# Residual rows of fifteen output tiles added by an accumulating DMA instead of by VectorE

## The reference, cut to what matters

```python
h = rms_norm(x, g_norm) * (1 + scale) + shift
p = h @ w_in                              # h_A, B_A, C_A, z_A, u_B, v_B, z_B, each 512 wide
s = c_a * h_a
y_a = b_a * dwconv3(s) * silu(z_a)
v_n = layer_norm(v_b, g_v, b_v)
y_b = u_b * chunk_spatial_mix(v_n, w_s, b_s) * silu(z_b)
y = concatenate([y_a, y_b]) @ w_out
out = rms_norm(x + gate * y, g_final)     # x is read a second time here: the residual
```

## Time and profile before

| what | before |
|---|---|
| median of 3 runs | 339.34 us |
| the profiled execution | 339.12 us |
| its span, slowest core (core 4) | 337.3 us (other cores 334.1 to 337.1) |
| TensorE busy | 284.2 us, 84% |
| VectorE busy | 187.7 us, 56% |
| ScalarE busy | 114.1 us, 34% |
| GpSimd busy | 110.7 us, 33% |
| TensorE's granted clock, mean of the core | 0.968 |

### The profile page before, as it was taken

The page is one execution under the profiler, slowest core; times in us unless marked ns, Lnnn a source line. Parts: engine busy times, 40 slices in busy tenths (PEclk is TensorE's granted clock), DMA queues, the critical chain, the costliest instruction groups (busy, mean ns, idle before and its releaser), DMA issues.

```text
span 337.3 us, 5476 instructions; the slowest of 8 cores (334.1 to 337.3 us)
## 1 busy us (share of the span) xinstructions
PE 284.2 (84%) x1696; PEld 147.6 (44%) x1720; DVE 187.7 (56%) x350; ACT 114.1 (34%) x206; POOL 110.7 (33%) x161
## 2 busy tenths in 40 slices
PE   0325539999899999998989999999999999999840
PEld 0222214444454444443445454445555557766420
DVE  0321015445564454277887857658864666668982
ACT  2611013206552234311824245543216242232320
POOL 7294055214523531141224435121432112223210
PEclk9999858999999999999999999999999999999995
DMA  6999999999999992339327444212670102426223
GB/s 136 209 174 168 156 162 155 169 173 256 206 234 223 173 141 57 103 82 247 127 103 211 110 172 149 64 54 76 121 249 3 31 2 106 143 69 208 86 108 126
DMA packets 23148, 46.72 MB, mean 139 GB/s; under 512 B 10960, under 2 KB 11344, under 8 KB 22096
## 3 DMA queue, kind: packets, MB, share of 16 engines
q0 software_dynamic: 6624, 21.24, 35.0%
q1 hardware_dynamic: 16496, 25.14, 25.4%
HBM read 51.02 MB, written 8.85 MB: 178 GB/s over the span
## 4 chain that ended last, share of the span: by engine, by line
PE 42%; DMA 29%; DVE 12%; issue 7%; ACT 3%; POOL 3%; SPq 1%; DVEq 1%; POOLq 0%; ACTq 0%
PE pb L486 26%; DMA win_bf<-win_l 12%; DMA wada<-wada_l 11%; PE pb L713 8%; PE pb L601 4%; DVE ob L811 3%; DMA xa<-x_p 2%; DMA xc<-x_p 2%; DVE tmp L541 2%; DVE st L616 1%; PE pb L823 1%; ACT tmp L534 1%; POOL xa L314 1%; DVE ob L729 1%; DVE ob L730 1%
## 5 line engine op out<-in xcount | busy, mean ns | idle before, releaser
L486 PE MATMUL pb<-hT,win_bf 128*128 128x512 bf16 (+3 forms) x672 | 125.1, 341 | 2.0 <-DMA win_bf<-win_l 1.4
L486 PEld LDWEIGHTS pb<-hT,win_bf 128*128 128x128 bf16 x680 | 66.0, 98 | 57.5 <-issue 2.7
L713 PE MATMUL pb<-wout_bf,yT 128*128 128x512 bf16 (+1 forms) x246 | 56.6, 379 | 3.4 <-POOL yT L685 1.2
L486 PE MATMUL pb<-hT,wh 128*128 128x512 bf16 (+3 forms) x277 | 54.0, 356 | 4.7 <-ACT hT L428 3.6
L560 POOL TENSOR_TENSOR yT<-tmp,tmp 128x512 bf16<-128x512 f32 (+3 forms) x20 | 23.3, 1164 | 61.0 <-DVE tmp L555 32.3
L486 PEld LDWEIGHTS pb<-hT,wh 128*128 128x128 bf16 x280 | 27.8, 100 | 29.7 <-issue 9.8
L685 POOL TENSOR_TENSOR yT<-tmp,tmp 128x512 bf16<-128x512 f32 (+3 forms) x20 | 22.0, 1098 | 51.5 <-DVE tmp L675 27.6
L541 DVE SCALAR_TENSOR_TENSOR tmp<-spad,pv,tmp 128x512 f32<-128x512 f32 (+2 forms) x40 | 26.2, 656 | 20.7 <-ACT tmp L534 13.5
L713 PEld LDWEIGHTS pb<-wout_bf,yT 128*128 128x128 bf16 (+1 forms) x256 | 23.9, 98 | 29.9 <-issue 2.9
L601 PE MATMUL pb<-wv_bf,hT 128*128 128x512 bf16 (+1 forms) x133 | 29.6, 379 | 0.2
L742 ACT ACTIVATE junk<-ob 128x1024 bf16<-128x1024 f32 (+1 forms) x16 | 16.9, 1053 | 38.0 <-DVE ob L732 37.9
(11 more groups left out here) (88 smaller groups left out, 252.9 us busy)
## 6 DMA issues: line engine op xcount, KB each, us to landing
y_p<-ob SPq DMA_DIRECT2D x15, 512.0 KB, 3.0
xc<-x_p SPq DMA_DIRECT2D x14, 512.0 KB, 6.9
wada<-wada_l POOLq DMA_DIRECT2D x6, 1024.0 KB, 35.4
xa<-x_p POOLq DMA_DIRECT2D x10, 512.0 KB, 39.1
win_bf<-win_l POOLq DMA_DIRECT2D x17, 256.0 KB, 42.7
xa<-x_p SPq DMA_DIRECT2D x8, 512.0 KB, 5.2
wout_bf<-wout_l POOLq DMA_DIRECT2D x2, 1024.0 KB, 57.7
wh<-winh_l POOLq DMA_DIRECT2D x4, 256.0 KB, 26.9
```

What stands on the lines that cost most here:

```text
L486: ii = pe.matmul(bk.t[:, 0:B.N], lhsT=wsl(m, k), rhs=hT[B.h][:, k, 0:B.N], start=(k == 0), stop=(k == 7))
L713: ii = pe.matmul(bk.t[R, :], lhsT=yT[B.y][:, k, ti * 128:ti * 128 + P], rhs=wout_bf[:, n, k, :], start=(k == 0), stop=(k == 7))
```

## The change

The residual of the 15 tiles of blocks 0 to 3 is no longer loaded into `xc` and added by VectorE. `C_s1` multiplies by the gate into `o` and then issues, from GpSimd's queue, a DMA that reads the residual rows in DRAM and adds them onto `o` in SBUF. The square waits for its landing. The two tiles of the last block keep the load on SP and the VectorE addition. The `xc` buffers go and `o` gets six buffers in place of three. The first instruction of `C_s2` moves from VectorE to GpSimd. In the last block `C_s3` of the previous block's last tile moves behind `C_s1` of the block's own tile 0.

```diff
-    NXC = 3
-    NOB = 3
-    xc = [A(f"xc{i}", [128, D], F32) for i in range(NXC)]
+    NOB = 6
...
-    def C_load(B, i, spare=None):
...
+    def C_load(B, i):
+        load("sp", xa[i][:], x_p[(B.t0 + i) * 128:(B.t0 + i + 1) * 128, :], ("xa", i))
+        cst[(B.i, i)] = [(xa[i], ("xa", i))]
...
     def C_s1(B, i, sq=True):
...
+        own = B.i == len(PB) - 1
...
         op("dve", fn, r=[b0.res, b1.res] + gr, w=[ores])
-        op("dve", lambda e: e.tensor_tensor(out=o[R, :], in0=o[R, :], in1=xt[R, :], op=ALU.add),
-           r=[ores, xr], w=[ores])
+        if own:
+            xt, xr = cst[(B.i, i)][0]
+            op("dve", lambda e: e.tensor_tensor(out=o[R, :], in0=o[R, :], in1=xt[R, :], op=ALU.add),
+               r=[ores, xr], w=[ores])
+        else:
+            src = x_s[0:64, :] if kind == "s" else x_p[(B.t0 + ti) * 128:(B.t0 + ti + 1) * 128, :]
+            op("pool", lambda e: e.dma_start(out=o[R, :], in_=src, accum_op=ALU.add), r=[ores], w=[ores], dma=True)
...
-        op("dve", lambda e: e.tensor_scalar(out=rs, in0=ss, scalar1=1.0 / D, scalar2=EPS, op0=ALU.mult, op1=ALU.add),
+        op("pool", lambda e: e.tensor_scalar(out=rs, in0=ss, scalar1=1.0 / D, scalar2=EPS, op0=ALU.mult, op1=ALU.add),
...
-    def C_step(B, i, nload=None):
+    def C_step(B, i):
...
-        if nload is not None:
-            C_load(*nload)
...
-            if j == 2 and b > 1:
-                first_c()
...
-                elif j < 4:
+                elif j < npv:
                     C_s3(PV, j - 1)
...
             C_s1(B, 0)
+            C_s3(PV, npv - 1)
             C_mm_half(B, 1, 0)
```

More of the change, by code:

```diff
@@ L706, in C_mm @@
         if k0 == 0:
-            cst[(B.i, i)] += [nbank(), nbank()]
-        b0, b1 = cst[(B.i, i)][1:3]
+            cst[(B.i, i)] = cst.get((B.i, i), []) + [nbank(), nbank()]
+        b0, b1 = cst[(B.i, i)][-2:]
         def fn(pe):
@@ L720, in C_s1 @@
         R = slice(64, 128) if kind == "s" else slice(0, 128)
-        (xt, xr), b0, b1 = cst[(B.i, i)]
+        own = B.i == len(PB) - 1
+        b0, b1 = cst[(B.i, i)][-2:]
         g = gate_s if kind == "s" else gate_p
@@ L985, in build_nc @@
         late = b < 2
-        def first_c():
-            for i in range(min(NXC, npv)):
-                C_load(PV, i)
         if last:
             for i in range(len(B.tiles)):
-                C_load(B, i, i)
+                C_load(B, i)
         for j in range(4):
@@ L1047, in build_nc @@
             gate_ada()
-            for q in range(NXC):
-                S.alias(("xc", q), [("wada", 0), ("wada", 1), ("wada", 2), ("xa", 4), ("xa", 5)])
             for q in range(NOB):
                 S.alias(("o", q), [("wada", 0), ("wada", 1), ("wada", 2), ("xa", 4), ("xa", 5)])
-            first_c()
         if not last:
@@ L1094, in build_nc @@
             if j < npv:
-                C_step(PV, j, (PV, j + NXC) if j + NXC < npv else None)
+                C_step(PV, j)
             if j == 2 and N2 is not None and b > 0:
```

## The result

The changed kernel takes 360.22 us in the median of 4 runs (359.39 to 360.75), against 339.32 us for the kernel before (4 runs, 338.82 to 340.24). The ratio is 1.060, with a 95% interval of 1.058 to 1.062. The spans of the cores are 350.7 to 358.5 us, where they were 334.1 to 337.3. Executions in which the cores of one die ran at a lower clock are left out of all times here.

What follows compares the result with a forecast made beforehand. TensorE's own work was taken to bound the kernel until 300 us, the chain over VectorE behind that. Terms 2.9 + 1.3 + 3.0 + 4.9 - 2.0 = 10.1 us on 339.1 gave 349 us, range 339 to 360.

Steps and rivals of the forecast that it cites:

- The landing L: Time from the accumulating DMA's issue to its landing: 5.3 us, between 3.7 and 7.1; half a us less for the sample tile.
- The handovers: Gaps between dependent instructions on different engines: two at a block's start, together 0.2 us.
- the ring: Last stretch: GpSimd's order chains transfer, square, root and next transfer; a turn takes 7.7 us, over the matmuls' 5.54.
- The gain of 2.0 us in block 1 and at the start of block 2: TensorE's two idle gaps behind VectorE's additions, 0.87 and 1.11 us, disappear; nothing if ScalarE holds the work back.
- Block 2: Block start: last tile's square delays the chain, and TensorE waits for a bank at projection U; cost L - 2.4 = 2.9 us.
- Block 3: Block start: same delay, tightest at the sixth matmul group near 255 us, slack 2.7; cost L - 4.0 = 1.3 us.
- Block 4: Block start, sample tile: no slack in the chain, 0.5 us saved by six buffers; cost L - 2.3 = 3.0 us.
- The tail: Last stretch: three landings in sequence, less the additions saved; cost 3L - 11.0 = 4.9 us.
- Squares inside a block: Blocks 1 to 3: the landing is hidden, with cover up to about 10 us; cost nothing.
- The slow landing: Rival: two reads at the rate of three loads in flight, landing 6.1 to 8 us, time 354 to 365; chance 0.22.
- The late starts are absorbed: Rival: delays in blocks 2 and 3 vanish in slack as VectorE has less to do; +5.9 us, 345 us; chance 0.2.
- The short landing: Rival: an accumulating transfer lands like a store, in 3.0 us; -2.8 us, 336 us; chance 0.12.

Runs made afterwards that it cites:

- late: Changed kernel with the square of each block's last tile, and the two steps behind it, emitted later in the next block; 345.3 us, ratio 1.014.
- tail: Changed kernel with block 3's three tiles, finished in the last block, back to a load and a VectorE addition; 352.4 us.
- noadd: Kernel before with the fifteen residual loads and additions left out, their result missing from the output; 337.8 us, ratio 0.995.
- late_tail: Changed kernel with the later squares and also block 3's three tiles added by VectorE again; 339.5 us, ratio 1.001.
- ring: Changed kernel with C_s2 of the previous tile emitted behind C_s1 of the current tile in the last block; 356.3 us.
- b_small: Kernel before with only two small edits: C_s2 wholly on GpSimd, and C_s3 behind C_s1 of the last block's tile 0; 339.3 us, ratio 0.999.
- plain: Changed kernel with the fifteen transfers copying the residual over the products without adding; 350.8 us, ratio 1.029.

## Why the prediction was wrong

The direction was right, with 0.80 on slower, and so was the main mechanism: landings that stand in the order of ScalarE and GpSimd, as late and tail show. The size was not: 349 us forecast, 360.2 measured, just past the end of the range. By its own steps:

- **The landing L, the failed step.** I took 5.3 us, "nearer to the lower" bound; it measures 6.1 as the mean of the eight cores' medians. Five of the six landings in the sum are of 512 KB, so this alone is worth 4.0 us; the sample tile landed after 4.7 us, and 4.8 was expected. The plain load by GpSimd lands after 4.5, not 3.7, and the accumulation adds 1.7. My lower bound was a row of another queue.
- **The handovers.** I allowed 0.1 us between the gate's product and the issue. At block 2 it is 0.55 us (172.18 to 172.73) and in the last stretch 0.61 (314.81 to 315.42). Some 0.5 us at each of three block starts and once at the first turn of the ring: 2 us.
- **The gain of 2.0 us in block 1 and at the start of block 2, the other failed step.** It isn't there in the median (+0.1 in block 1; noadd 0.0 there, and -0.2 in block 2). The two gaps of the earlier trace rows are those of core 4. Five of the eight cores have the same 32.9 us in block 1 and no gap over 0.16 us, as core 0 of the kernel before, TensorE's rows on either side of the block's end:

```profile
164.56 3.63 PE L713 MATMUL pb<-wout_bf,yT 128*128 128x512 bf16 x16
168.02 4.33 PE L486 MATMUL pb<-hT,wh 128*128 128x448 bf16 x22
```

- Cores 3 and 4, which had gaps, do get 1.5 and 0.9 us faster in block 1 of noadd. On core 4 of the changed kernel the two gaps shrink from 1.98 to 0.44 us, but four other cores get a new one of 0.56 to 1.47 us (above, under late_tail). That is the case for which the prediction itself had put the gain at nothing: ScalarE holds L653 back.
- **Block 2.** L - 2.4 with the measured L and the handover gives 4.2; measured 5.3. The sum went by core 4, where the gate's second product ended 5.0 us into the block, the latest of all cores (1.8 to 5.0, median 3.9). In the changed kernel it ends 5.7 us into it on six of eight. Core 7, two rows of before and four of the changed kernel (block 2 starts at 166.21 and at 167.04):

```profile
168.05 0.68 DVE L730 TENSOR_TENSOR ob<-pb,gate_p 128x512 f32<-128x512 f32 x1
...
171.33 0.51 ACT L515 COPY tmp<-pb 128x448 f32<-128x448 f32 x1
```

```profile
166.09 0.91 POOL L729 DMA_DIRECT2D ob<-x_p  x1 [0.67 <-ACT hT L426]
...
169.51 0.75 DVE L387 TENSOR_SCALAR xn<-xa,stat 128x1024 bf16<-128x1024 f32 x1 [1.51 <-POOL stat L380]
...
172.04 0.68 DVE L721 TENSOR_TENSOR ob<-pb,gate_p 128x512 f32<-128x512 f32 x1
...
180.49 0.51 ACT L513 COPY tmp<-pb 128x448 f32<-128x448 f32 x1
```

  So the copy of H starts 13.45 us into the block, where it started at 5.1: 8.3 us late (6.8 in the median of the cores), not the 5.3 that the sum gives with the measured L and the handover. The block follows it: from this copy to the start of block 3 it is 51.4 us on five cores of the changed kernel, early copy or late (11.4 to 13.9 us into the block). The gate's product is late because it stands on VectorE behind L387, which waits 1.51 us for a root (L380) that GpSimd runs behind the accumulating issue and `C_s2`. The prediction had left this root out of what stands behind an issue. This is read from the rows; no run isolates it. Nor does TensorE stall at U first, where I had counted: it stalls at the banks of H and B, and at U only for the last 0.9 us.
- **The clock behind the stall** had no term in the sum either, but it isn't what block 2 lacks. Busy time by stretch of the changed kernel, core 4 (the last three columns are the granted clock, the DMA share and GB/s), and TensorE's rows of core 7:

```profile
184.00:186.00 2.00, 0.01 (x1) 0.04 (x2) 2.00 (x4) 0.16 (x1) 1.80 (x2) 0.99 0.00 0
186.00:190.00 4.00, 4.00 (x13) 1.69 (x14) 2.74 (x8) 2.45 (x6) 2.34 (x3) 0.58 0.67 197
190.00:194.00 4.00, 3.95 (x20) 1.86 (x20) 3.90 (x7) 0.29 (x1) 3.21 (x3) 1.00 0.32 119
```

```profile
181.14 3.19 PE L484 MATMUL pb<-hT,win_bf 128*128 128x448 bf16 x16 [1.48 <-ACT tmp L513]
186.53 3.19 PE L484 MATMUL pb<-hT,win_bf 128*128 128x448 bf16 x16 [2.20 <-DVE tmp L553]
```

  Behind the two gaps core 4's granted clock is 0.58, close to the lower of its two levels, and the 16 matmuls there take 4.83 us in place of 3.19; cores 5 and 6 show the same (4.87 and 4.86). Core 7 has the same two gaps, its clock stays at 1.00 and the matmuls take 3.19, as on cores 1 and 3. These three lose 5.7, 5.1 and 5.5 us in block 2, cores 4 to 6 lose 4.7, 5.8 and 6.1. From the copy of H to block 3 the cores with the lower clock need 52.0 us, the others 51.4. So the clock costs 0.6 us, not the 1.6 by which the matmuls are longer: at full clock TensorE waits 0.9 us for the bank at U later on, and with the slower matmuls it doesn't.
- **Block 3.** L - 4.0 + 0.5 = 2.6; measured 2.3, and that is in part luck. From the issue to the square it is 6.6 to 7.2 us here, while the gate's product comes 0.7 us earlier in the block than before (1.56 us in, was 2.23), and TensorE stalls at the bank of B (1.84 us, at 247.08 on core 4), not near 255. **Block 4.** The sample tile lands after 4.7 us in the mean of the cores, so 4.7 - 1.85 + 0.5 = 3.4; measured 3.1. **The tail.** 3 x 6.1 - 11.0 + 0.5 = 7.8; measured 6.8 over the two stages that it covers. The ring is not the whole mechanism of the last: in ring, 4.0 of the 6.8 us go with GpSimd's order.
- **Sum.** 10.1 + 4.0 for L + 2 for the handovers + 2.0 for the absent gain is 18, and the medians of the stages give 18 (block 2 has 1.1 more than its term, the tail, blocks 3 and 4 together 1.6 less). The slowest core's span grew by 21.2 (337.3 to 358.5), since core 6 lost 6.1 in block 2, 4.2 in block 4 and 1.8 in block 1. I had worked on one core; the metric is the slowest of eight, whose spans now lie 7.8 us apart in place of 3.2.
- **Squares inside a block, six buffers, `C_s2` on GpSimd, the moved `C_s3`:** costed at nothing. For the last two b_small shows nothing, and late_tail, with all of them in, is as fast as before in the median of the cores; the squares inside block 1 are not free on every core.
- **The rivals.** The slow landing, 354 to 365 us with a chance of 0.22, is the one that came. "The late starts are absorbed" is refuted by the table and by late; its argument took 12.47 of 20 us for VectorE's densest stretch, while the page of before shows five slices of 8.4 us with VectorE at 80 to 90% between 160 and 245 us. The short landing is refuted by the transfers' rows. The rule that an add in the DMA path costs a second read gave up to 360 us. The Trainium skill ("Collectives: The Full Stack", "The bandwidth ceiling: the fold count and why AG ≠ RS ≠ AR") states it for a ReduceScatter and was right in the direction here; the part that goes with the bytes grows 1.6 times, not twice.

## What to carry to other kernels

Moving 18 us of additions off an engine that isn't the limit is worth at most what leaving them out is worth (here 1.6 us), and a DMA in a chain of dependences costs its whole landing wherever the next instruction in line waits for it. So ask first who waits for the landing and what stands behind that waiter on its engine: squares moved to a later place gave back 15 of 21 us, with every landing as long as before. And check on the other cores that a gap counted as gain is there, and where the chain starts on them.

## What the runs showed of the hardware

- An accumulating DMA from GpSimd's queue, 128 rows of 4 KB: issue 0.91 us, landing 6.1 us; without the addition 0.63 and 4.5. At 128 rows of 1 KB: 0.91 and 3.5, against 0.61 and 2.9.
- A plain load of 512 KB issued by SP landed after 3.7 us on an otherwise quiet queue; issued by GpSimd (plain, core 4) after 3.5 us at the least, and 4.5 in the mean of the cores' medians.
- Behind gaps of 1.5 to 1.9 and then 2.2 us with 3.19 us of matmuls between them, TensorE's granted clock fell on cores 4, 5 and 6 (0.58 on core 4 from 186 to 190 us, 1.00 again after that) and stayed at 1.00 on cores 1, 3 and 7, in one execution. Where it fell, 16 matmuls took 4.83 to 4.87 us in place of 3.19, and the block grew by 0.6 us.
